# S5 input projected by channel tiles among the GLA passes and regrouped into chunks through DRAM, and a reordered plain segment of the second feed-forward layer

## What is computed

```python
x = ffn_sublayer(x, ...);  ctx = ffn_sublayer(ctx, ...)
u, q, k, v, r, glr, ga, gb = split(h @ w_in)        # h: normalised tokens; u: 512 channels, the S5 input
ya = s5_branch(u_lat, u_ctx, ...)                   # 32 groups of 16 channels, 64 complex states, two directions
yb = gla_branch(q, k, v, r, glr, ...)               # gated linear attention, chunks of 64 tokens, two directions
y  = (sigmoid(ga) * (ya @ s5_out) + sigmoid(gb) * (yb @ gla_out)) @ w_o
x  = x + gate * y;  x = ffn_sublayer(x, ...);  out = rms_norm(x)
```

## Time and profile before

| | us |
|---|---|
| median of 3 runs | 1453.16 (1452.70 to 1455.42) |
| the profiled execution | 1456.54 |
| its span | 1454.8 |
| TensorE busy | 1423.2 (98%) |
| weight loads on TensorE | 1272.9 (87%) |
| DVE, ACT, GpSimd busy | 839.9, 392.3, 638.4 |

### The profile page before, as it was taken

The page is one execution under the profiler, slowest core; times in us unless marked ns, Lnnn a source line. Parts: engine busy times, 40 slices in busy tenths (PEclk is TensorE's granted clock), DMA queues, the critical chain, the costliest instruction groups (busy, mean ns, idle before and its releaser), DMA issues.

```text
span 1454.8 us, 21292 instructions
## 1 busy us (share of the span) xinstructions
PE 1423.2 (98%) x8560; PEld 1272.9 (87%) x8560; DVE 839.9 (58%) x1290; ACT 392.3 (27%) x722; POOL 638.4 (44%) x403
## 2 busy tenths in 40 slices
PE   7999999999999999999999999999999999999998
PEld 3699999999999999987898888888898799999996
DVE  2774467467554554246536539714767756665566
ACT  3320010010010010023635231124122254555454
POOL 1363443433433533413620446633747264656652
PEclk9999999999999999999999999999999899999999
DMA  9532353353335334114310168375665143333422
GB/s 350 160 109 64 118 147 108 113 139 112 117 99 152 98 117 141 44 33 131 89 30 1 44 183 224 123 221 169 196 174 172 31 117 88 94 110 94 128 73 83
DMA packets 227933, 174.43 MB, mean 120 GB/s; under 512 B 28632, under 2 KB 202876, under 8 KB 227836
## 3 DMA queue, kind: packets, MB, share of 16 engines
q1 hardware_dynamic: 208656, 142.50, 33.6%
q10 hardware_dynamic: 19180, 30.58, 6.5%
HBM read 155.26 MB, written 17.79 MB: 119 GB/s over the span
## 4 chain that ended last, share of the span: by engine, by line
PE 88%; DVE 6%; ACT 2%; issue 2%; DMA 1%; POOL 0%; SPq 0%; DVEq 0%; POOLq 0%; ACTq 0%
PE ps L1082 43%; PE ps L1712 12%; PE ps L1337 9%; PE ps L1773 4%; PE ps L1340 4%; PE ps L1091 2%; PE ps L1114 2%; PE ps L1434 2%; PE ps L1289 1%; PE ps L1170 1%; PE ps L1179 1%; PE ps L1587 1%; DVE h_lo L3218 1%; DVE ada_acc L2482 1%; PE ps L1541 1%
## 5 line engine op out<-in xcount | busy, mean ns | idle before, releaser
L1004 POOL TENSOR_SCALAR w_hi<-w_raw 128x1024 fp32r<-128x1024 f32 (+1 forms) x131 | 154.2, 1177 | 634.2 <-PE ps L1082 363.7
L1007 POOL TENSOR_TENSOR w_lo<-w_raw,w_hi 128x1024 fp32r<-128x1024 f32 (+1 forms) x131 | 321.8, 2456 | 10.9
L1082 PE MATMUL ps<-h_hi,w_lo 128*128 128x384 f32 (+2 forms) x936 | 269.5, 351 | 0.0
L1082 PE MATMUL ps<-h_hi,w_hi 128*128 128x384 f32 (+2 forms) x936 | 266.2, 348 | 0.0
L1082 PE MATMUL ps<-h_lo,w_hi 128*128 128x384 f32 (+2 forms) x936 | 266.1, 348 | 0.0
L1082 PEld LDWEIGHTS ps<-h_hi,w_lo 128*128 128x128 f32 x936 | 167.8, 189 | 12.8 <-issue 2.9
L1082 PEld LDWEIGHTS ps<-h_hi,w_hi 128*128 128x128 f32 x936 | 169.5, 189 | 9.3
L1082 PEld LDWEIGHTS ps<-h_lo,w_hi 128*128 128x128 f32 x936 | 169.6, 189 | 9.2
L1064 POOL TENSOR_TENSOR w_lo<-w_raw,w_hi 128x512 fp32r<-128x512 f32 x90 | 115.3, 1294 | 112.8 <-ACT w_hi L2257 111.1
L2482 DVE SCALAR_TENSOR_TENSOR ada_acc<-ada_w,cs,ada_acc 128x1024 f32<-128x1024 f32 x70 | 110.5, 1610 | 10.6 <-DMA ada_w<-in_ada_w_dram 8.4
L1916 ACT ACTIVATE silu<-ps 128x768 f32<-128x768 f32 (+1 forms) x26 | 20.3, 780 | 325.6 <-PE ps L1082 316.5
(11 more groups left out here) (421 smaller groups left out, 3049.3 us busy)
## 6 DMA issues: line engine op xcount, KB each, us to landing
w_raw<-in_ffn_w_gate_dram SPq DMA_DIRECT2D x44, 512.0 KB, 4.8
w_raw<-in_ffn_w_up_dram SPq DMA_DIRECT2D x44, 512.0 KB, 4.0
w_raw<-in_ffn_w_down_dram SPq DMA_DIRECT2D x42, 512.0 KB, 4.3
ada_w<-in_ada_w_dram ACTq DMA_DIRECT2D x32, 512.0 KB, 4.1
w_raw<-in_w_in_dram SPq DMA_DIRECT2D x32, 512.0 KB, 4.0
ada_w<-in_ada_w_dram SPq DMA_DIRECT2D x30, 512.0 KB, 4.7
c_scr<-cp ACTq DMA_DIRECT2D x16, 288.0 KB, 3.9
b_scr<-bt_sb ACTq DMA_DIRECT2D x16, 256.0 KB, 4.0
```

What stands on the lines that cost most here:

```text
L1004: pool.tensor_scalar(w_hi[:, s, 0:cols], w_raw[:, s, 0:cols], 1.0, 1.0, ALU.mult, ALU.mult)\
L1007: pool.tensor_tensor(w_lo[:, s, 0:cols], w_raw[:, s, 0:cols], w_hi[:, s, 0:cols].bitcast(F32), ALU.subtract).then_inc(w_split, 1)
L1082: last = pe.matmul(mv[2], st, mv[part], start=(first and q == 0), stop=(n == len(terms) - 1 and q == 2))
```

## The change

- The four u units become channel tiles (`tall`, like q, k, v). Eight parts take the place of the eight u jobs: part 2q is tile q over the 512 latent tokens, part 2q+1 the same tile over the 256 context tokens, each with the channels as stationary side. Unit q is free after part 2q+1.
- ACT copies a part into `u_t` with the tokens ordered by place in the chunk, reversed, and after every second part stores tile q (384 KB) to a DRAM buffer `u_scr` from its own queue.
- SP loads `ut` from it with 32 transfers, 8 for each tile: 16 partitions, 8 groups, runs of 96 numbers (384 B). They wait for all four stores and for the last readout job, and stand in SP's list before the stream load b = 3.
- The transposing jobs "ut" are gone, `CHUNK_ORDER` begins with two r jobs, and xs jobs 0, 2, 4 and 6 wait for the loads of their tile.
- ACT's square root of the GLA norm moves from the fourth "ut" job to the second r job.
- In the plain segment T tile 0 is added up at f = 0, split at f = 1, T tile 3 is added up at f = 3, and T tiles 2 and 3 are split at the first two down jobs; the ada tiles are divided 3, 4, 1, 0 over f (they were 3, 3, 2, 0) with some behind the T tile's work; ACT rounds T tile 1 in f = 3 before it waits for the product of that tile, and not in f = 2; the weight sums come at down job 3 (before: 5), the first low part made by DVE at 6 (before: 7).

```diff
-              ("v", 4), ("u0", 1), ("vt", 6), ("gla", GLA_JOBS), ("chunks", 32), ("gb", 8), ...
+              ("v", 4), ("u0", 1), ("vt", 6), ("gla", GLA_JOBS), ("chunks", 24), ("gb", 8), ...
-CHUNK_ORDER = [("ut", 4), ("r", 1), ("ut", 4), ("r", 1), ("xs", 6), ("r", 1), ("xs", 6), ("r", 1), ("ybt", 4), ("xs", 4)]
+CHUNK_ORDER = [("r", 2), ("xs", 6), ("r", 1), ("xs", 6), ("r", 1), ("ybt", 4), ("xs", 4)]
...
     if UNIT["u"] <= n < UNIT["u"] + 4:
-        return GJ["u", CH - 1]
+        return GJ["u", 2 * (n - UNIT["u"]) + 1]
...
-            wide(UNIT["u"], C_U)
+            tall(UNIT["u"], 4, C_U)
             tall(UNIT["r"], 4, C_R)
...
+            def chunk_inputs(q):
+
+                for t in range(CH):
+                    src = bass.AP(u_scr.tensor, (q * P * CH + t) * NCH, [[CH * NCH, GC], [GC * CH * NCH, 8], [1, NCH]])
+                    sp.dma_start(ut[GC * t:GC * t + GC, 8 * q:8 * q + 8, :], src).then_inc(ut_here[q], 16)
+
             for b in range(8):
+                if b == 3:
+                    sp.wait_ge(u_out, 4 * 16)
+                    is_done(sp, GJ["out", 3] + 3)
+                    for q in range(4):
+                        chunk_inputs(q)
                 if b >= 3:
                     is_done(sp, CJ["xs", 2 * (b - 3) + 1])
...
+            def input_part(p):
+
+                q, j = p // 2, GJ["u", p]
+                n, c = UNIT["u"] + q, slice(NL, NT) if p % 2 else slice(0, NL)
+                if p % 2 == 0:
+                    pe.wait_ge(w_split, n + 5)
                 wait_read(pe, j)
+                wh, wl = wv(n % 4, KD, P)
+                split_mm([(wh[:, k, :], wl[:, k, :], [(h_hi[:, k, c], h_lo[:, k, c], lat(j)[:, 0:c.stop - c.start])])
+                          for k in range(KD)]).then_inc(job_done, 1)
...
             def state_inputs(b, j):
 
-                if b == 0:
-                    for q in range(4, 8):
-                        was_read(pe, CJ["ut", q])
+                if b < 8 and b % 2 == 0:
+                    pe.wait_ge(ut_here[b // 2], 16 * CH)
...
                         if n == NT:
                             dst, src = dst.rearrange("p (b c) -> p b c", b=2), both(ju, 384)
+                        if blocks_of_h and f == SEG - 1:
+                            tile_hi(1)
                         act.wait_ge(gu_ok, i * SEG + (act_base + part.segs * SEG + f + 1))
...
-            def take_u(s):
-                j = GJ["u", s]
+            def take_u(p):
+                q, j = p // 2, GJ["u", p]
+                c = slice(LCH, NCH) if p % 2 else slice(0, LCH)
                 is_done(act, j)
-                act.activation(u_tok[:, :, CH - 1 - s, :], lat(j)[0:NCH, :].rearrange("p (g c) -> p g c", c=GC), ACT.Copy)\
-                    .then_inc(slot_read[j % 4], 1)
+                by_place = lat(j)[:, 0:CH * (c.stop - c.start)].rearrange("p (n t) -> p t n", t=CH)
+                act.activation(u_t[:, q, :, c], by_place[:, ::-1, :], ACT.Copy).then_inc(slot_read[j % 4], 1)
+                if p % 2:
+                    was_read(act, GJ["u", p - 1])
+                    was_read(act, j)
+                    act.dma_start(u_scr[q], u_t[:, q, :, :]).then_inc(u_out, 16)
...
-                for t in ((), (0,), (1,), (2, 3))[f]:
+                for t in ((), (0,), (), (2, 3))[f]:
                     tile_hi(t)
...
-                if f_ == 1:
+                if f_ == 0:
                     dve.wait_ge(h_copied, 2)
                     add(1, 0, 0, 0, sub)
                     add(1, 1, 0, 1)
                     add(1, 1, 0, 0, sub, last=True)
+                elif f_ == 1:
+                    low(0)
                 elif f_ == 2:
-                    low(0)
...
                     add(1, 1, 1, 0, last=True)
-                elif f_ == SEG:
                     dve.wait_ge(h_copied, 4)
                     add(0, 0, 0, 1, sub)
-                elif f_ == SEG + 1:
-                    add(0, 1, 1, 1)
-                elif f_ == SEG + 2:
-                    add(0, 1, 0, 1, sub, last=True)
+                    add(0, 1, 1, 1)
+                    add(0, 1, 0, 1, sub, last=True)
+                elif f_ == SEG:
+                    low(2)
+                elif f_ == SEG + 1:
+                    low(3)
                 elif f_ == SEG + 3:
-                    low(2)
-                    low(3)
-                elif f_ == SEG + 5:
                     weight_sums(0)
-                elif f_ == SEG + 7:
+                elif f_ == SEG + 6:
                     low_ahead(block_of("group", 0, 2))
...
-                            for k in range(*ada[f_]):
+                            for k in range(*((0, 2), (3, 6), (7, 8), (8, 8))[f_]):
                                 ada_add(ADA_MIX + 1, k)
                             tiles_of_h(f_)
+                            for k in ((2,), (6,), (), ())[f_]:
+                                ada_add(ADA_MIX + 1, k)
```

More of the change, by code:

```diff
@@ L190 @@
               ("ffn1", FFN1_JOBS), ("norm1", 0), ("q0", 1), ("q1", 1), ("glr", 1), ("k", 2), ("z0", 1), ("z1", 1),
-              ("v", 4), ("u0", 1), ("vt", 6), ("gla", GLA_JOBS), ("chunks", 32), ("gb", 8), ("ga", 8), ("merge", len(MERGE_ORDER)),
+              ("v", 4), ("u0", 1), ("vt", 6), ("gla", GLA_JOBS), ("chunks", 24), ("gb", 8), ("ga", 8), ("merge", len(MERGE_ORDER)),
               ("ma", KD), ("wo", KD), ("ada7", 1), ("wo_b", 4), ("ffn2", FFN2_JOBS),
@@ L317, in build @@
     x_scr = nc.dram_tensor("x_scr", [P, KD, NL], F32).ap()
+    u_scr = nc.dram_tensor("u_scr", [4, P, CH, NCH], F32).ap()
     g_scr = nc.dram_tensor("g_scr", [P, 2 * KD, NL], F32).ap()
@@ L389, in build @@
     u_at = m[0]
-    u_tok = mix("u_tok", [NCH, G, CH, GC])
+    u_t = mix("u_t", [P, 4, CH, NCH])
+    m[0] = u_at + 4 * G * CH * GC
     ut_at = m[0]
@@ L722, in build @@
         sum_lo = sem("sum_lo")
+        u_out = sem("u_out")
+        ut_here = [sem(f"ut_here{q}") for q in range(4)]
         block_hi = sem("block_hi")
@@ L868, in _ @@
             w_in = a["w_in"][0].rearrange("(k p) c -> p k c", p=P)
-            def wide(n, c0):
-                for q in range(4):
-                    unit(n + q, w_in[:, 2 * q:2 * q + 2, c0:c0 + 512], raw((n + q) % 4, 2, 512))
             def tall(n, count, c0, c=P):
@@ L1413, in tall_job @@
                 split_mm(tall_terms(name, q, j, toks, c)).then_inc(job_done, 1)
-            def wide_job(name, j, cols, rows):
-                n = UNIT[name]
-                wait_read(pe, j)
[L1419 to L1427, removed]
+            def input_part(p):
[3 more added lines that the diff above has]
+                    pe.wait_ge(w_split, n + 5)
+                wait_read(pe, j)
+                wh, wl = wv(n % 4, KD, P)
+                split_mm([(wh[:, k, :], wl[:, k, :], [(h_hi[:, k, c], h_lo[:, k, c], lat(j)[:, 0:c.stop - c.start])])
+                          for k in range(KD)]).then_inc(job_done, 1)
             def latents(name, q, j, c, k0, k1):
@@ L1483, in _ @@
                 tall_job("v", q, JOB["v"] + q, NT)
-            wide_job("u", GJ["u", 0], lambda h, k: h[:, k, 0:NT:CH], NCH)
+            input_part(0)
             for q in range(4):
@@ L1562, in _ @@
                 else:
-                    wide_job("u", GJ["u", p], lambda h, k: h[:, k, p:NT:CH], NCH)
-            def turn_u(b, j):
-                if b == 0:
[L1568 to L1574, removed]
+                    input_part(p)
             def state_inputs(b, j):
-                if b == 0:
-                    for q in range(4, 8):
-                        was_read(pe, CJ["ut", q])
+                if b < 8 and b % 2 == 0:
+                    pe.wait_ge(ut_here[b // 2], 16 * CH)
                 if b % 2 == 0:
@@ L1599, in _ @@
             for name, b, j in CHUNK_JOBS:
-                if name == "ut":
-                    turn_u(b, j)
-                elif name == "ybt":
+                if name == "ybt":
                     turn_o(b, j)
@@ L1904, in ada_tile, with ffn @@
                 act.dma_start(ada_w[:, s, :], ada_src(g, k)).then_inc(ada_here[s], 16)
-            def ffn(jobs, parts, n, act_base, blocks_of_h=None):
+            def ffn(jobs, parts, n, act_base, blocks_of_h=None, tile_hi=None):
                 def seg(part, i):
@@ L2105, in _ @@
                 is_done(act, j)
[L2106 to L2109, removed]
+                if name == "r":
+                    if b == 1:
                         act.wait_ge(o_rs, 1)
                         act.activation(oms[:, :], oms[:, :], ACT.Sqrt, bias=eps[:, :], scale=1.0 / DV).then_inc(o_rs, 1)
-                elif name == "r":
                     act.activation(r_sb[:, b, :], lat(j), ACT.Silu).then_inc(slot_read[j % 4], 1)
@@ L2221, in blocks_of_h @@
                     copy_h(f // 3)
-                for t in ((), (0,), (1,), (2, 3))[f]:
+                for t in ((), (0,), (), (2, 3))[f]:
                     tile_hi(t)
-            ffn(JOB["ffn2"], PARTS2, NL, FF // P, blocks_of_h)
```

(1 more changed line is left out.)

## The result

| | before | after |
|---|---|---|
| median of 5 runs, us | 1453.71 (1452.70 to 1455.42) | 1447.12 (1443.20 to 1447.44) |
| profiled execution, its span | 1456.54, 1454.8 | 1443.20, 1441.5 |
| TensorE busy | 1423.2 | 1408.7 |

The account below looks back on a forecast made before the run. The last chain was taken as 88% TensorE, so work removed there counts fully. Gains of 7.2 (passes), 0 (chunk stage) and 7.7 us (plain segment) sum to 14.9: 1453.2 - 14.9 = 1438.3 us, range 1431 to 1447.

Parts of the forecast that it names:

- Part 1a: S5 projection on TensorE: 14.1 us less before the last readout, 2.8 us less behind it as the transposes go.
- Part 1b without contention: GLA passes: shorter context parts expose waits on DVE and ACT of 2.9 to 3.0 us, GpSimd's splits left aside.
- Part 1b, contention in cumulate(2): GLA passes: GpSimd's split after context part 1 lengthens DVE's cumulate(2) by 0.7 us, so readout(1) waits 0.8 us.
- if the split in cumulate(2) costs 3 us on the path as well: Lower bound for the passes: that split costs 3 us on the path, leaving a gain of 4 us.
- the clock falls in the passes: Rival: a 3 us wait around short products halves TensorE's clock, u(6) costs 4.7 us more, 1443.0 us; 14%.
- The later waits: GLA passes: TensorE waits 3.05 us at keys(3), 1.0 behind scores(3), 0.5 at key_values(2) and 0.9 at readout(3).
- Part 1c: Chunk stage: 32 input loads issued every 0.63 us, third tile 2.6 to 3.1 us late; worth 0.
- +2.8 us (issues of 0.43 us): Upper bound for the chunk stage: loads issued every 0.43 us leave a gain of 2.8 us.
- The rival that put the loads on the slower side: Input loads choke SP at 1.35 us an issue, 1461.0 us, 5%; at 0.94 us an issue 1448, 5%.
- Part 2: Plain segment: new DVE and ACT order removes the ada wait and the clock fall; gain 7.7 us, bounds 3.1 and 8.0.
- The doubling for short runs: Chunk input loads: read-modify-write of runs under 512 B might double a transfer to 0.94 us, making the stage some 10 us longer.

Follow-up runs that it names:

- e1: The changed kernel with GpSimd's four splits of r weights again waiting for the last input part, as before the change; 1438.69 us, ratio 0.9877.
- e6: The changed kernel with 12 of the 24 products of latent part 4 made twice, as extra TensorE work ahead of readout(1); 1444.53 us, ratio 0.9928.
- e3: The kernel before with only the plain segment's edits, the S5 input as before; 1450.21 us, ratio 0.9954.
- e8: The kernel before with only DVE's part of the plain segment's edits (additions and ada tiles in the new order); 1449.42 us, ratio 0.9964.
- e7: The kernel before with only ACT's part of the plain segment's edits (rounding of T tile 1 behind silu(3)); 1451.71 us, ratio 0.9979.
- e4: The changed kernel run again unaltered, for a second profile and five more times; 1447.88 us, ratio 0.9938.
- e5: The changed kernel with only the first split of r weights early, the other three waiting for the last input part; 1437.23 us, ratio 0.9878.
- e2: The kernel before with only the S5 input change, the plain segment as before; 1454.08 us, ratio 0.9983.
- e10: The changed kernel with the first two splits of r weights early, the last two waiting for the last input part; 1446.85 us, ratio 0.9940.
- e9: The kernel before with only the S5 input change, all four splits of r weights waiting for the last input part; 1442.10 us, ratio 0.9921.

## Why the prediction was wrong, and where it was right

The direction was right; the size was less than half. By its own steps:

- **Part 1a, TensorE's removed work: near.** Four parts of 5.71 and four of 3.05 us are 35.0, where 33.6 were summed, so 12.7 us go and not 14.1. The transposes went as told, and the chunk stage is 2.7 us shorter.
- **Part 1b without contention: near.** e1 shows the walk with GpSimd idle: waits of 0.5 at key_values(1), none at readout(1) ("arrives even"), 0.3 at key_values(2), 1.0 behind scores(3) and 0.8 at readout(3), 2.6 in all; 2.9 were summed. The passes gained 9.1 us, with the 0.35 of part 0 9.5; the forecast without contention was 11.2: 1.4 of the gap is the length of the parts.
- **Part 1b, contention in cumulate(2): the step that failed.** The prediction put "+0.7 us" on the split behind context part 1 and gives no working for it; it is near the 0.81 us by which ke outlasted its split. What ke lost in the same rows was 2.2 us (3.15 in place of 0.95), and the prediction charged that to ke of pass 3 but not to cumulate(2). Two operations with both inputs in SBUF stood under this split, L2931 and then the scan, and they lost 0.61 and 2.03 us; the scan ended at 766.21, 1.6 us after the split's end at 764.60. These 2.64 us are the wait at readout(1): 2.61 us, where 0.8 was forecast and e1 has none. The prediction kept "if the split in cumulate(2) costs 3 us on the path as well" as a bound, and priced it at 3 us only.
- **What it set off, and the larger part of the miss: the clock, which the sum put at nothing.** The rival "the clock falls in the passes" is what happened, with a chance of 14%, but at another place and at another price. It was put at u(6) and priced by 24 products, 4.7 us. It came at readout(1), a readout being the longest run of short products in the passes. The halved clock cost 6.2 us there, 0.7 in the transposes and 0.9 in the scores: 7.8 us. The three waits of the changed kernel are 3.9. 12.7 less 7.8 less 3.9 is 1.0, beside 0.6 in the profile. The rows that spoke against the rival, 1.88 us of 4 busy at clock 1.00, did not bear the weight given to them: with 1.83 of 4 it fell here.
- **The later waits were right for a kernel that didn't come about.** The waits at keys(3) (3.05), behind scores(3) (1.0) and at key_values(2) (0.5) vanish in the changed kernel, as TensorE is late itself. e1 and e6 show them: 1.0 and 0.3 there, 2.9 at keys(3) here.
- **Part 1c: the issue step was mis-sized.** 0.475 us in place of 0.63, so that the loads were never late and the 2.8 us of the transposes stayed a gain of 2.7. This was the bound "+2.8 us (issues of 0.43 us)". The rival that put the loads on the slower side had no part in it.
- **Part 2: right in size and mechanism.** No ada wait, clock 1.00 through 1114 to 1146, 0.57 us at the fourth down job (0.35 forecast), the blocks without a wait for x: 7.1 us in the profile where 7.7 were forecast, and 6.4 to 6.7 in e3. The prediction named ACT's order as the cause behind most of it; e8 shows that DVE's order alone keeps the clock up and gains 5.2 us, and ACT's alone (e7) 2.9.

Put right with these sizes, the sum is 0.6 + 2.7 + 7.1 = 10.4 us for this profile, and 9.0 for that of e4; the medians say 6.6 and 8.8. The two profiles of the changed kernel differ by 2.8 us ahead of the mixer, which is most of the difference for this one.

What stays open is why the clock fell in some stretches and not in others; the runs show where, and no rule that fits all of them (below). A version that starts the r splits early and keeps them off the scan in another way than by waiting was not tried; e1 and e5 (1438.7 and 1437.2 us) are faster than both kernels.

## What to carry to other kernels

When a buffer is given back earlier, look at what the engine that refills it will then run beside: here the refill itself was on nobody's path, and it lay on the one DVE operation without slack. Price a wait of a few us not by its length alone: if the clock falls, all that TensorE runs until it rises again takes longer (1.8 times, by the readout's steps and the scores). Here 2.6 us of waiting in front of the readout cost 7.8 us more, and 2.9 us in front of the key transposes (e6) 2.8 more, where the next job of 512-column products came sooner. That such products bring the clock back sooner than short ones is not shown: near 1132 us in the kernel before it stayed at 0.50 for 10 us of them, with two more waits in between. And measure the contention on the operation that stands there, not on a neighbour.

## What the runs showed of the hardware

- **DVE's scan under a GpSimd split:** `TENSOR_TENSOR_SCAN` of 128x768 with both inputs in SBUF takes 1.76 us alone and 3.79 to 3.81 under a split; a two-input addition of the same size 0.96 and 1.57, ke 0.95 and 3.09. The scan and ke lose nearly what they share with the split's second half, the one with two inputs: the scan lost 2.03 of the 2.18 us from 762.42 to 764.60, ke in e6 2.14 of the 2.28 from 789.52 to 791.80. The first half, with one input, isn't free either: qz in e5 lost 0.83 us and shared only 0.45 with the second half. Seven state updates with one input in PSUM took 2.76 us with and without one. The Trainium skill ("SBUF — State Buffer", Who interferes with whom) says that a DVE instruction with two SBUF inputs contends with a GpSimd instruction that reads SBUF, and that one with at most one, outside the modes that use two ports, doesn't. The traces agree, for the scan too.
- **Which waits bring the clock down.** At readout(1), with a wait of 2.61 us, the clock fell to 0.50 in the changed kernel, in e2, e4 and e10. At readout(3), with 0.80 us, it fell in none of them, nor in e1, e5, e6 and e9. Behind scores(3), with 1.0 us, it didn't (e1). At keys(3), with 2.9 us, it did (e6). With 1.25 us (before) and 1.50 us (e7) in front of the one-column products it did; with 1.27 us some 3 us behind them it didn't (e8).
- **Small loads in a row:** 32 loads of 48 KB to 16 partitions, in runs of 384 B, were issued every 0.475 us and each landed 1.9 to 2.2 us after its issue, so none piled up. The Trainium skill ("SBUF — State Buffer", Door 1: The DMA port swizzle) gives 104 GB/s for 16 partitions; by the windows from 820 to 832 us these loads moved 101 to 106 GB/s, which that figure fits. No run here shows whether the queue or the ports set the 0.475. The doubling for short runs that the prediction weighed did not show: it would have been 0.94 us a load.
- **ACT reading PSUM at a stride:** the copies that turn the order of the tokens took 0.60 us for 512 columns and 0.38 for 256, as long as plain ones:

```profile
753.97 0.60 ACT L2044 ACTIVATE u_t<-ps 128x512 f32<-128x512 f32 x1 [6.79 <-PE ps L1092]
```
